# Half of the gate and up products of one SwiGLU layer as seven half-unit products for eight, with sums of weights from GpSimd

## The reference, cut to what matters

```python
D_MODEL = 2048
SEQ = 256
FFN_HIDDEN = -((-8 * D_MODEL) // (3 * 256)) * 256      # 5632

def swiglu(x, w_gu, w_d):
    gate, up = jnp.split(x @ w_gu, 2, axis=-1)
    return (jax.nn.silu(gate) * up) @ w_d
```

## Time and profile before

| | |
|---|---|
| Median of 3 runs | 3443.3 us (3443.24 to 3444.61) |
| The profiled execution | 3443.67 us |
| Span in that profile, first to last instruction | 3441.9 us |
| Mean granted clock of PE | 0.999 of full speed |
| The loop over chunks 2 to 9 | 8 trips |

### The profile page before, as it was taken

How to read it: one execution, slowest core, us unless ns; L and a number is a source line. 1 busy time by engine, 2 the same in 40 slices (tenths; PEclk the granted TensorE clock), 3 DMA queues, 4 the chain that set the end, 5 groups by cost and what they waited for, 6 DMA issues and landing times.

```text
span 3441.9 us, 42740 instructions
## 1 busy us (share of the span) xinstructions
PE 3426.8 (100%) x15844; PEld 2808.4 (82%) x15844; DVE 1944.3 (56%) x2315; ACT 1609.9 (47%) x2063; POOL 302.9 (9%) x418
## 2 busy tenths in 40 slices
PE   9999999999999999999999999999999999999999
PEld 8788878888888888777888878888888788888887
DVE  4544575555555755667556545567544845555546
ACT  5444444444444455454444444446556644444443
POOL 0000010000000000002343303000380000000000
PEclk9999999999999999999999999999999999999999
DMA  7555565556556455456555547655554555655554
GB/s 247 167 169 180 200 205 189 191 183 195 191 186 195 159 172 159 129 195 169 187 188 196 189 159 217 208 194 163 192 173 151 167 187 185 195 185 188 188 186 144
DMA packets 333316, 630.11 MB, mean 183 GB/s; under 512 B 33180, under 2 KB 36096, under 8 KB 331648
## 3 DMA queue, kind: packets, MB, share of 16 engines
q1 hardware_dynamic: 326272, 603.20, 54.7%
q0 software_dynamic: 6768, 25.05, 2.3%
q10 hardware_dynamic: 144, 0.07, 0.0%
HBM read 624.86 MB, written 2.33 MB: 182 GB/s over the span
## 4 chain that ended last, share of the span: by engine, by line
PE 97%; DVE 2%; ACT 1%; issue 0%; DVEq 0%; POOL 0%; ACTq 0%; POOLq 0%
PE psum L269 29%; PE psum L271 28%; PE psum L270 28%; PE psum L323 3%; PE psum L601 1%; PE psum L603 1%; PE psum L602 1%; PE psum L938 1%; PE psum L951 0%; PE psum L3136 0%; PE psum L519 0%; PE psum L517 0%; PE psum L518 0%; DVE weights_lo L230 0%; PE psum L3156 0%
## 5 line engine op out<-in xcount | busy, mean ns | idle before, releaser
L230 DVE TENSOR_TENSOR weights_lo<-weights_raw,weights_hi 128x1024 fp32r<-128x1024 f32 (+1 forms) x1139 | 1398.1, 1237 | 1202.5 <-ACT weights_hi L217 1201.7
L217 ACT CAST weights_hi<-weights_raw 128x1024 fp32r<-128x1024 f32 (+1 forms) x1139 | 1195.0, 1052 | 1656.1 <-PE psum L271 1644.2
L269 PE MATMUL psum<-weights_hi,act_hi 128*128 128x512 f32 x3048 | 1210.9, 397 | 0.1
L271 PE MATMUL psum<-weights_hi,act_lo 128*128 128x512 f32 x3048 | 1189.4, 390 | 0.0
L270 PE MATMUL psum<-weights_lo,act_hi 128*128 128x512 f32 x3048 | 1187.3, 390 | 0.0
L271 PEld LDWEIGHTS psum<-weights_hi,act_lo 128*128 128x128 f32 x3048 | 572.0, 188 | 122.5
L269 PEld LDWEIGHTS psum<-weights_hi,act_hi 128*128 128x128 f32 x3048 | 572.6, 188 | 121.4 <-issue 8.9
L270 PEld LDWEIGHTS psum<-weights_lo,act_hi 128*128 128x128 f32 x3048 | 573.1, 188 | 112.9
L269 PE MATMUL psum<-weights_hi,hid_hi 128*128 128x512 f32 x1320 | 517.4, 392 | 0.0
L271 PE MATMUL psum<-weights_hi,hid_lo 128*128 128x512 f32 x1320 | 514.1, 389 | 0.0
L270 PE MATMUL psum<-weights_lo,hid_hi 128*128 128x512 f32 x1320 | 513.7, 389 | 0.0
(11 more groups left out here) (452 smaller groups left out, 1934.4 us busy)
## 6 DMA issues: line engine op xcount, KB each, us to landing
weights_raw<-in_ffn_wgu SPq DMA_DIRECT2D x344, 512.0 KB, 4.3
weights_raw<-in_w_ff SPq DMA_DIRECT2D x252, 512.0 KB, 3.9
weights_raw<-in_ffn_wd SPq DMA_DIRECT2D x176, 512.0 KB, 3.6
weights_raw<-in_even_w_in SPq DMA_DIRECT2D x120, 512.0 KB, 3.5
weights_raw<-in_w_in SPq DMA_DIRECT2D x64, 512.0 KB, 3.5
weights_raw<-in_odd_w_in SPq DMA_DIRECT2D x60, 512.0 KB, 3.7
weights_raw<-in_odd_w_o SPq DMA_DIRECT2D x32, 512.0 KB, 3.6
weights_raw<-in_w_out SPq DMA_DIRECT2D x32, 512.0 KB, 3.7
```

What stands on the lines that cost most here:

```text
L217: nc.scalar.copy(w_hi[:, u % SPLIT_SLOTS, done:size], raw[:, u % RAW_SLOTS, done:size]).then_inc(hi_ready, 1)
L230: nc.vector.tensor_tensor(w_lo[:, u % SPLIT_SLOTS, done:size], raw[:, u % RAW_SLOTS, done:size], w_hi[:, u % SPLIT_SLOTS, done:size].bitca ...
L269: nc.tensor.matmul(o, ah, wh, start=(k + j == 0), stop=False)
L271: last = nc.tensor.matmul(o, al, wh, start=False, stop=(k + j == kts - 1))
```

## The change

Chunks 2 to 9 of the first layer are computed in another way. The other three chunks keep the steps as they were.

**Seven products for eight.** For the first 8 of the 16 k tiles, the two token halves, two halves of these k tiles (0 to 3 and 4 to 7) and the gate and up columns form a 2 x 2 by 2 x 2 product of blocks. The change computes it with the seven products of Strassen's scheme in Winograd's form, P1 to P7. Each product is two **half-units**: a 512 KB piece of (summed) weights against one token half, 6 matmuls instead of 12. The token side needs five sums (`side_sums`, once, on POOL and ACT). The weight side needs four sums of 2 units per chunk (`column_sums`), on POOL, in place in SBUF: P5 = a + b, P7 = b + d, P6 = a + b + d and P4 = a + b + d + c, where a, c are the gate pieces of the two k halves and b, d the up pieces. k tiles 8 to 15 go on as full units.

**Items.** A step is now 22 items and the 8 down units. The items in order: P1 (2 half-units), gate 4, P2 (2), P5 (2), gate 5, gate 6, P6 (2), gate 7, P3 (2), P7 (2), P4 (2), up 4 to up 7. That makes 14 half-units and 16 full ones, 276 matmuls, with 30 high and 30 low parts instead of 24. Gate and up are put together from PSUM and snapshots of it: 4 copies on ACT, 4 small additions and the final product on DVE.

**Slots.** There are 5 split slots during these steps. The raw slots are split up: 4 in a ring for the plain units, 2 each for a, b, c, d. The pieces of the next chunk (a, a, b, b, d, d, c, c) are loaded between D0 to D7, and those into c and d wait for `sides_low`, since their buffers first hold the token sums.

**Evacuations** take both halves in one instruction of 2 x 512 everywhere but in one place (`by_half`).

```diff
+ITEMS = [("P1", 0), ("P1", 1), ("gate", 4), ("P2", 0), ("P2", 1), ("P5", 0), ("P5", 1), ("gate", 5), ("gate", 6),
+         ("P6", 0), ("P6", 1), ("gate", 7), ("P3", 0), ("P3", 1), ("P7", 0), ("P7", 1), ("P4", 0), ("P4", 1),
+         ("up", 4), ("up", 5), ("up", 6), ("up", 7)]
+SUMS = [("P5", 0), ("P5", 1), ("P7", 0), ("P7", 1), ("P6", 0), ("P6", 1), ("P4", 0), ("P4", 1)]
...
+    def slot_load(sp, c, slot, src, cols, unit):
+        nk = src.shape[1]
+        if slot in c.user:
+            sp.wait_ge(lo_ready, c.until(c.user[slot] + 1))
+        sp.dma_start(raw_at[slot][:, :nk * cols].rearrange("p (k n) -> p k n", n=cols), src).then_inc(landed[slot], 16)
...
+    def high_part(act, c, of, size):
+        to = c.split_slot()
+        if to in c.user:
+            act.wait_ge(w_used, c.until(c.user[to] + 1))
...
-        for m in range(TT):
-            last = do(m, dst(m), psum[:, 2 * pair + m, :])
+        if by_half:
+            for m in range(TT):
+                last = do(m, dst(m), psum[:, 2 * pair + m, :])
+        else:
+            both = slice(0, TT)
+            last = do(both, dst(both), psum[:, 2 * pair:2 * pair + 2, :])
...
+                if x in "cd":
+                    sp.wait_ge(ready("sides_low"), 2)
+                user = {"a": "P4", "b": "P7", "c": "P4", "d": "P7"}[x]
+                slot_load(sp, c, QUAD[x] + q, rows(w1, k, 2, col), BLK, base + ITEM[user, q])
...
+            def down(ch, base, quads):
+                for u in range(8):
+                    slot_load(sp, c, c.raw_slot(), rows(w2, ch * kts + 2 * (u % 2), 2, (u // 2) * BLK), BLK, base + u)
+                    if u < len(quads):
+                        quads[u]()
...
+        def side_sums():
...
+            pool.wait_ge(ready("sides_high"), 2)
+            for p in ("P5", "P6", "P7", "P3"):
+                last = G.tensor_tensor(side_lo[p][:], side_whole[p][:], side_hi[p][:].bitcast(F32), ALU.subtract)
+            last.then_inc(ready("sides_low"), 1)
+
+        def column_sums():
...
+                for p, q in SUMS:
+                    a, b, c_, d = (raw_at[QUAD[x] + q] for x in "abcd")
+                    if p == "P5":
+                        landing("a", q)
+                        landing("b", q)
+                        pool.wait_ge(lo_ready, unit + ITEM["P1", q] + 1)
+                        ins = G.tensor_tensor(a, a, b, ALU.add)
+                    elif p == "P7":
+                        landing("d", q)
+                        ins = G.tensor_tensor(b, b, d, ALU.add)
+                    elif p == "P6":
+                        pool.wait_ge(lo_ready, unit + ITEM["P5", q] + 1)
+                        ins = G.tensor_tensor(a, a, d, ALU.add)
+                    else:
+                        landing("c", q)
+                        pool.wait_ge(lo_ready, unit + ITEM["P6", q] + 1)
+                        ins = G.tensor_tensor(a, a, c_, ALU.add)
+                    ins.then_inc(ready("summed"), 1)
...
+                def sides(u):
+                    if u != 19:
+                        return
...
+                def behind(i):
+                    if i == 0 and before is None:
+                        add_at(base - 4, start - 3, 1)
+                    if i == 2 and before is None:
+                        add_at(base - 2, start - 2, 2)
+                    if i == 4:
+                        if before is None:
+                            add_at(base, start - 1, 3)
...
+                    if i in (8, 13):
+                        turn_taken(0 if i == 8 else 2)
+                    if i == 17:
+                        gate_whole(0)
+                    if i == 22:
+                        gate_whole(1)
+                    if i == 25:
+                        up_whole()
+                    if i == 28:
+                        add_at(base + 24, start + 2, 0)
```

More of the change, by code:

```diff
@@ L183, in ready @@
     def ready(name):
+        name = SHARED.get(name, name)
         if name not in named:
@@ L1015, in ffn_body @@
         n = 16 + 4 * len(units_of(kts, 512))
-        return {"unit": n, "block": 6, "turn": kts // 2, "split_turn": kts // 2, "hidden_h": 2 if kts == 8 else 0}
+        return {"unit": n, "block": 6, "turn": kts // 2, "split_turn": kts // 2, "hidden_h": 2 if kts == 8 else 0,
+                "ring": n, "split": n} | {f"raw{i}": n // RAW_SLOTS for i in range(RAW_SLOTS)}
     def fused(E, link, out, in0, scalar, in1, op0, op1, tmp):
@@ L2740, in beside, with sums_low, step @@
+            def sums_low(after):
+                after = step(1, after, True, at_down=lambda: c.rings(range(4)))
+                c.rings(None, range(SPLIT_SLOTS + 1))
+                sums_step(after)
+                with c.loop(dve, SUMS_TRIPS, sums_per):
+                    sums_step(None)
+                sums_step(None, True)
+                c.rings(None, range(SPLIT_SLOTS))
+            def step(ch, before, first_outs, passed=False, also=None, at_down=None):
                 def beside(u):
@@ L3212, in hidden @@
             step(None, 0)
             step(c.n["block"] - 1, 2)
-            for n_loop, trips in enumerate(loops_of(which, n)):
+            if which == 0:
+                pe.wait_ge(ready("sides_low"), 2)
+                c.rings(None, range(SPLIT_SLOTS + 1))
+                sums_step()
+                with c.loop(pe, SUMS_TRIPS, sums_per):
+                    sums_step()
+                sums_step()
+                c.rings(None, range(SPLIT_SLOTS))
+            for n_loop, trips in enumerate(loops_of(which, n)) if which else ():
```

372 lines of the change are left out of this document (326 added, 46 removed).

## The result

| | before | after |
|---|---|---|
| Median | 3443.95 us (4 runs) | 3497.12 us (4 runs, 3493.74 to 3499.22) |
| Span of the profiled execution | 3441.9 us | 3494.9 us |
| Ratio | | 1.0154, 95% interval 1.0141 to 1.0166 |

The change costs 53 us where 18 were forecast. The direction was right; the size lies outside the range, which ended at 3477.

What follows compares the result with a forecast made beforehand. PE was taken to bound the kernel, busy 3426.8 of 3441.9 us. Matmuls -21.8, port +21, loads +7 and way in +11 gave +18 on 3443.67, so 3462 us, range 3430 to 3477.

Steps and rivals of the forecast that it cites:

- part 3: Loads between D0 and D7: D6's data land late, PE waits before D4, +1.06 us per step, seven times, +7.
- Part 1: Sums steps: 276 matmuls for 288, -2.72 us for each of eight chunks, -21.8 us.
- Part 2: Gate 5 to P3: POOL's additions and DVE's low parts take turns at the port, +2.6 us per step, +21.
- Rival 1: Port does not take turns: DVE keeps it through rows of low parts; about 3448 us, chance 0.13.
- rival 2: POOL's additions are as fast as L1080, 1.96 us with hold 1.80; 3432 us, chance 0.12.
- rival 3: All is hidden but the way in, the port costs nothing PE sees; 3426 us, chance 0.08.
- rival 4: Worse: bursts at 370 GB/s or additions of 2.5 us; 3470 to 3479 us, chance 0.17.
- Part 4: Way in, plain to first sums step: c and d loads wait for token sums; +6.4 before D5, +5 after, +11.
- +5 in the first sums step: First sums step: DVE enters without its lead, sums begin about 6 us later against PE, +5 us.
- Parts that cost nothing: ACT's extra high parts and snapshots hidden; merged evacuations save about 0.06 us each, at the norms -1 to +1 us.

Runs made afterwards that it cites:

- e10: e8 with the split slots turned, (4, 1, 2, 3, 0) in the sums steps and (1, 2, 3, 0) behind them: 3425.82 us, ratio 0.9946 to before.
- e11: e10 with the eight weight sums back on POOL instead of DVE: 3455.31 us, ratio 1.0035 to before.
- e3: Changed kernel with the product of gate and up, and ACT's second Silu, behind D2 instead of D3: 3496.56 us, ratio 1.0155 to before.
- e5: Changed kernel with SP's loads reordered in the sums steps: D0 to D3, a, b, D4 to D7, d, c: 3482.72 us, ratio 1.0114 to before.
- e2: Changed kernel with ACT's six copies of the token sums behind unit 3 instead of 19 of the second step: 3484.20 us, ratio 1.0116 to before.
- e8: Changed kernel with sums on DVE, edits of e3 and e5 (way in too), token side spread with early copies, POOL's loads moved: 3432.28 us, ratio 0.9967.
- e9: Changed kernel with only the split slots' order turned, (4, 1, 2, 3, 0), then (1, 2, 3, 0): 3492.02 us, ratio 1.0138 to before.

## Why the prediction was wrong, point by point

The largest step that failed is part 3: its overlap of the loads with D0 to D7 had too early a landing and looked at one wait of two. It missed 2.1 us in each of seven steps. Beside it the sum left out POOL's own work and loads at both ends of the layer (6.2 and 3.0 us) and the restarted slots (4.5 us), and the way in was mis-sized by 4.7 us.

**Part 1, the matmuls**: 96 fewer, as said. Their worth was put a little high: e10 has a step of 63.92 without any wait, where 63.54 was counted. -18.7 us for the eight, not -21.8. The surplus goes mostly with the fifth split slot, and not with half-units: in e10's sums steps, matmuls whose weights lie in the fifth slot start 231 to 233 ns apart on the mean, the others 227 to 228, and D3, a full unit in that slot, takes 2.79 us for 2.72. A fifth of 276 matmuls at 4 to 5 ns is about 0.25 of the 0.38 us. Why that slot is slower was not tried.

**Part 2, the port**: right in mechanism, place and size inside the loop. Turns are taken there; an addition is 2.41 us alone; the waits are before gate 5, gate 7 and P3. In the step shown P3 begins 25.3 us behind P1, as worked out, and 22.9 in e10 (22.7 in the prediction). Of these 2.4 us the idle time is 1.45; the rest is what each restart costs besides, which the prediction did not have. Turns are no rule, though: at the start of the layer POOL's first four additions ran through without one. Rival 1 (DVE keeps the port) and rival 2 (additions of 1.96) fall by the rows of the loop, and rival 3 (no cost that PE sees) by PE's waits. So does rival 4 as a mechanism, though its 3470 to 3479 came nearest: additions are not 2.5, and the bursts run at 380 to 395 GB/s.

**Part 3, the loads behind the down units**: the step that failed inside the loop, with 2.1 us per step (69.45 against the 67.36 of e11). Two things were missing. The rate of 391 GB/s was taken from the burst's first byte on, but it took some 4 us to get there (15, 227 and 314 GB/s in stretches of 2 us). So D3 landed at T+46.8 and not T+44.8, and D6 at T+55.0 and not T+52.9; from D3 on the loads land 1.36 us apart, near the 1.34 assumed. And D2 was not looked at, only D4. By the prediction's own numbers D3 lands at T+44.8; high part, low part and the 2.6 us of the product make it T+49.7; PE wants D2 at T+49.8. There was a margin of 0.1 us, and the burst's start took it. Why a burst begins slowly was not tried. e3 shows that mending the product alone only hands the wait on to D4, and e5 that the loads' order is worth 2.0 us per step. And in the step shown (679.03 to 748.75, so 69.72, 5.8 more than e10's) the five waits are 3.95 in sum: each cost 0.37 us besides, on the mean. 0.16 of it is the reading: the idle time counts from the end of the last matmul, 0.39 us behind its start, where the next would have started 0.23 behind. The first weight load begins with its matmul instead of 0.23 us ahead, the next matmul starts 0.34 us later for 0.23, and the ones that follow are slower for a while.

**Part 4, the way in**: the mechanism was right, as e2 shows, and the size was short. The wait before D5 was 8.3 us for 6.4: D3's raw data landed 3.6 us later than assumed, and POOL's four subtractions took 6.0 us where 8.9 were allowed. The slow clock behind the wait was not in the sum, so that e2 takes 11.1 us from the way in. The other 4.5 us (e8 to e10; 5.1 in e9) are a term that the prediction did not have. The split slots are counted from 0 anew as the sums begin, and slot 0 is the one that D7, the unit just before, is using. ACT idles 6.4 us for it and PE 2.5. It could be read in the whole diff: `rings` sets the counter back. The "+5 in the first sums step" came near by luck: that step was 5.2 us longer than its followers, but not by the wait on the way in, as the prediction has it. e2 takes that wait away, e9 the one for the slot, and the step stays at 74.4 and 74.3; e11 has neither and keeps 3.9. There the sums do begin 6 us late against PE, as was said, but behind an addition onto x in DVE's list. That this addition is the cause is read from the trace and not shown by a run.

**Parts that cost nothing**: this held for the evacuations (in e10 the start takes 38.3 us as before, and the distance behind the last batch is 44.5 in both) and for ACT. But the list left out POOL's own work ahead of the additions, eight operations on the token side. They were costed as delay of `sides_low`, never as a hold of the port. At the start of the layer, with DVE four low parts short of a lead, that cost 6.2 us, 5.05 of them as a wait of PE. And POOL's loads of the next mixer, which stand behind the sums in its queue, came 635 us later, on top of the last down loads: 3.0 us. The queue of every engine that a step is moved past has to be gone through, and POOL's was not.

**Sum of what was missed**: 6.2 (start) + 4.5 (slots) + 11.1 - 6.4 (way in) + 7 x 2.1 (D2 and the burst, with the first sums step) + 3.0 (end) = 33 of the 35 us. The rest is part 1's 3 us, less what the port took below its forecast.

## What to carry to other kernels

- Before handing work of DVE to POOL, compare how long POOL's instruction holds the port with how long DVE would need for it. Here 2.27 against 1.14 us: the offload cost more of DVE's time than the work did, and 3.4 to 5 us per step of PE's.
- A wait that is added where an engine has no lead (a layer's first units, a slot ring that is started over) costs its full length; the same operations of POOL 6.5 us later were free. Go through the first and last trips of a loop apart from its middle, and through every engine's queue.
- When one resource is late, list all that stands within a microsecond or two of being late behind it. The first wait that is mended hands its time to the next (e3), so mend them together (e8, e10), and judge the change by that.
